# Samples' state products of an mLSTM and a GLA mixer: key and value parts stacked along the contraction, one float32r product of 96 rows in place of row-tiled float32 ones

## The reference, cut to what matters

```
C_new = decay[..., None, None] * C + jnp.einsum('bshd,bshv->bhdv', kw, vc)             # mLSTM
S_new = jnp.exp(BL)[..., None] * S + jnp.einsum('bshd,bshv->bhdv', kc * jnp.exp(BL[:, None] - Bc), vc)   # GLA
```

## Time and profile before

| | |
|---|---|
| median of 3 runs | 2538.49 us (2538.44 to 2538.94) |
| the profiled execution | 2539.21 us, span 2537.4 |
| TensorE busy | 2517.5 us, 99% |
| VectorE busy | 1675.8 us, 66% |
| ScalarE busy | 1072.3 us, 42% |
| products of L1656 (both layers) | 128 records |
| first block of layer 0, of layer 1 | near 568, near 1925 us |

### The profile page before, as it was taken

The page is one execution under the profiler, slowest core; times in us unless marked ns, Lnnn a source line. Parts: engine busy times, 40 slices in busy tenths (PEclk is TensorE's granted clock), DMA queues, the critical chain, the costliest instruction groups (busy, mean ns, idle before and its releaser), DMA issues.

```text
span 2537.4 us, 40969 instructions
## 1 busy us (share of the span) xinstructions
PE 2517.5 (99%) x16901; PEld 2276.0 (90%) x16901; DVE 1675.8 (66%) x2654; ACT 1072.3 (42%) x1568; POOL 0.2 (0%) x4
## 2 busy tenths in 40 slices
PE   9999999999999999999999999999999999999998
PEld 7899898887888999889998998998887988999998
DVE  6744575556457673357764778677876478888886
ACT  5343445442334442454533344446543344433333
POOL 0000000000000000000000000000000000000000
PEclk9999999999999999999999999999999999999999
DMA  6455544535433433453323343344436433333332
GB/s 227 138 173 162 148 150 141 156 110 178 146 102 119 137 96 100 154 170 109 96 84 125 117 135 119 123 155 141 122 106 191 145 129 117 88 100 100 96 100 100
DMA packets 176709, 330.41 MB, mean 130 GB/s; under 512 B 19964, under 2 KB 93436, under 8 KB 176524
## 3 DMA queue, kind: packets, MB, share of 16 engines
q1 hardware_dynamic: 176524, 327.79, 41.2%
HBM read 271.46 MB, written 56.28 MB: 129 GB/s over the span
## 4 chain that ended last, share of the span: by engine, by line
PE 91%; DVE 5%; ACT 2%; issue 1%; DMA 0%; SPq 0%; ACTq 0%; DVEq 0%
PE ps L1192 68%; PE ps L1320 10%; PE ps L1206 3%; PE ps L1570 1%; DVE Y L2438 1%; PE ps L1224 1%; PE ps L1512 1%; PE ps L1656 1%; DVE w_lo L2165 1%; PE ps L1501 1%; PE ps L1495 1%; ACT w_hi L1692 1%; PE ps L1374 1%; PE ps L1494 0%; PE ps L1603 0%
## 5 line engine op out<-in xcount | busy, mean ns | idle before, releaser
L1192 PE MATMUL ps<-HH,w_lo 128*128 128x288 f32 (+1 forms) x2680 | 902.4, 337 | 0.2 <-DVE w_lo L2165 0.2
L1192 PE MATMUL ps<-HL,w_hi 128*128 128x288 f32 (+1 forms) x2680 | 892.2, 333 | 0.0
L1192 PE MATMUL ps<-HH,w_hi 128*128 128x288 f32 (+1 forms) x2680 | 891.8, 333 | 0.0
L2165 DVE TENSOR_TENSOR w_lo<-w_stage,w_hi 128x1024 fp32r<-128x1024 f32 x392 | 478.4, 1221 | 178.3 <-ACT w_hi L1692 177.2
L1192 PEld LDWEIGHTS ps<-HH,w_lo 128*128 128x128 f32 x2680 | 502.9, 188 | 48.8 <-issue 5.8
L1192 PEld LDWEIGHTS ps<-HL,w_hi 128*128 128x128 f32 x2680 | 502.8, 188 | 42.7
L1192 PEld LDWEIGHTS ps<-HH,w_hi 128*128 128x128 f32 x2680 | 503.0, 188 | 41.6
L1692 ACT ACTIVATE w_hi<-w_stage 128x1024 fp32r<-128x1024 f32 x392 | 412.1, 1052 | 295.8 <-PE ps L1192 257.2
L1192 PE MATMUL ps<-hid_hi,w_lo 128*128 128x288 f32 (+1 forms) x1052 | 346.8, 330 | 1.9 <-DVE Y L2438 1.1
L1192 PE MATMUL ps<-hid_lo,w_hi 128*128 128x288 f32 (+1 forms) x1052 | 343.8, 327 | 0.0
L1192 PE MATMUL ps<-hid_hi,w_hi 128*128 128x288 f32 (+1 forms) x1052 | 343.6, 327 | 0.0
(11 more groups left out here) (336 smaller groups left out, 3271.5 us busy)
## 6 DMA issues: line engine op xcount, KB each, us to landing
w_stage<-w_gate_in SPq DMA_DIRECT2D x88, 512.0 KB, 3.7
w_stage<-w_up_in SPq DMA_DIRECT2D x88, 512.0 KB, 3.7
w_stage<-w_down_in SPq DMA_DIRECT2D x88, 512.0 KB, 3.7
w_stage<-w_in_in SPq DMA_DIRECT2D x80, 512.0 KB, 4.1
w_stage<-w_out_in SPq DMA_DIRECT2D x32, 512.0 KB, 3.8
proj_scratch<-evicted SPq DMA_DIRECT2D x48, 288.0 KB, 2.3
proj_scratch<-evicted SPq DMA_DIRECT2D x32, 256.0 KB, 2.1
w_stage<-w_v_in SPq DMA_DIRECT2D x16, 512.0 KB, 4.3
```

The source lines that it names most:

```text
L1192: mm = pe.matmul(ps[:, grp.bank + t, 0:W], wsl(w, k), x[:, k, t * W:(t + 1) * W], start=(k == first and m == 0), stop=(k == last and m == 2))
L2165: dve.tensor_tensor(g.wlo[:, n % NW, :], g.wst[:, n % NW, :], g.whi[:, n % NW, :].bitcast(F32), ALU.subtract).then_inc(s["w_lo"], 1)
```

## The change

Each layer gets two stacks of three thirds of 32 rows: `K4` (high, high, remainder of the weighted keys, for both halves e) and `V4` (high and remainder of the values, so placed that each third of the product is high x high, high x low or low x high). ScalarE makes the high thirds in `key_parts` and `value_parts`, 4 copies each, VectorE the remainders in `prepare(layer, 0)`, 2 and 2. `prepare` masks both halves' stacked keys in one operation per piece, into `k_batch`, whose second buffer lies in `proj_sums`. L1656 becomes one float32r product of 96 rows at full tile per piece and half: 4 per block as before, without a tile position. New waits: ScalarE for its own copies of keys and values, VectorE for all 8 high parts (`parts_hi`) ahead of the remainders and so of the batches of j = 0, TensorE for `parts_lo` ahead of the first L1656 of a layer.

```
--- before.py
+++ after.py
@@ -546,6 +546,8 @@
     g.S1H = sb("s1_hi", [P, 512], F32R)
     s1 = nc.sbuf_base
     g.S1 = sb("s1", [P, 512])
+    g.V4 = nc.alloc_sbuf_tensor_at("v_parts", [3 * 4 * DS, 2, H, DV], F32R, offset=s1 - 3 * 2048)
+    g.K4 = nc.alloc_sbuf_tensor_at("k_parts", [3 * 4 * DS, 2, H, P], F32R, offset=t_end)
     g.S1L = nc.alloc_sbuf_tensor_at("s1_lo", [P, 512], F32R, offset=s1)
     g.Y = [sb(f"Y{b}", [P, KD, NT[b]]) for b in range(2)]
     g.wst = sb("w_stage", [P, NW, 1024])
@@ -554,7 +556,9 @@
     g.hh = sb("hid_hi", [P, 2, NT[1]], F32R)
     g.hl = sb("hid_lo", [P, 2, NT[1]], F32R)
     g.E = sb("evicted", [P, 3, NT[1]])
+    up = nc.sbuf_base
     g.UP = sb("proj_sums", [P, 2, GW[1]])
+    g.KB1 = nc.alloc_sbuf_tensor_at("k_batch_odd", [3 * 4 * DS, 2, 2, P], F32R, offset=up)
     g.C = sb("state", [P, H, DV + 1])
     g.ident = sb("ident", [P, P])
     g.ones = sb("ones", [P, P])
@@ -565,7 +569,7 @@
     g.RC = sb("rstd_column", [P, 4])
     g.mask = sb("mask", [P, L])
     g.mask8 = sb("mask8", [TS, TS])
-    g.bmr = sb("batch_rows", [TS, NB + NB // 2])
+    g.bmr = sb("batch_rows", [3 * 4 * DS, NB + NB // 2])
     g.lmask = sb("level_masks", [P, NLV * L // 2 + L], U32)
     g.reset = sb("reset", [P, L + TS])
     g.bi = sb("bias_if", [H, 2])
@@ -613,7 +617,7 @@
     m.YN = piece("m", "y_normed", [P, H, DV])
     m.TT = piece("m", "y_gated", [P, KD, L])
     m.QB = piece("m", "q_batch", [P, 4, P])
-    m.KB = piece("m", "k_batch", [TS, 4, P])
+    m.KB = piece("m", "k_batch", [3 * 4 * DS, 2, 2, P], dt=F32R)
     m.CS = piece("m", "sample_state", [P, CRING, 2, DV + 1], at["m"])
     at["m"] += 4 * 2 * (DV + 1) * 4
     m.QK = piece("m", "qk", [P, 2 * H, L])
@@ -637,7 +641,7 @@
     x.XL = piece("l", "levels", [P, NLV, H, L])
     x.CS = piece("l", "sample_state", [P, CRING, 2, DV], levels)
     x.QB = piece("l", "q_batch", [P, 4, P], levels + 12288)
-    x.KB = piece("l", "k_batch", [TS, 4, P], 0)
+    x.KB = piece("l", "k_batch", [3 * 4 * DS, 2, 2, P], 0, F32R)
     x.AS = piece("l", "sample_scores", [TS, H, P], 2048)
 
     g.PT = nc.dram_tensor("proj_scratch", [28, P, T], F32, kind="Internal").ap()
@@ -667,7 +671,7 @@
     "n_ready", "spread", "qb_zeroed", "qb", "kb", "b_inter", "b_state", "b_added", "n_saved", "keys_summed", "half_yn", "half_sq", "half_ln", "half_est",
     "half_small", "outs", "y_stored",
 
-    "sums", "s_hi", "s_lo", "t_sum", "t_hi", "t_lo", "prod", "silu", "gated", "p_silu",
+    "sums", "s_hi", "s_lo", "t_sum", "t_hi", "t_lo", "prod", "silu", "gated", "p_silu", "parts_hi", "parts_lo",
 )
 RINGS = (("w_landed", NW), ("x_landed", KD), ("stored", 3), ("c_landed", CRING), ("c_stored", CRING))
 
@@ -681,7 +685,18 @@
     ps = g.ps
     M0 = 4
 
-    BY_ROWS = ((0, 0), (32, 0))
+    def k_batch(layer, j):
+
+        return (g.x if layer else g.m).KB if j % 2 == 0 else g.KB1
+
+
+
+    V_HIGH = ((0, 2), (1, 2))
+    V_LOW = (1, 0)
+
+    def third(r):
+
+        return slice(32 * r, 32 * r + 32)
 
     def normed(N, k):
 
@@ -1627,7 +1642,7 @@
                 if j == NB - 1 and not layer:
 
                     for i in range(H):
-                        mm = pe.matmul(ps[:, M0, 288 + i * NB:288 + (i + 1) * NB], x.KW[0:TS, i, :], g.bmr[:, 0:NB],
+                        mm = pe.matmul(ps[:, M0, 288 + i * NB:288 + (i + 1) * NB], x.KW[0:TS, i, :], g.bmr[0:TS, 0:NB],
                                        start=True, stop=True)
                     mm.then_inc(s["keys_summed"], 1)
                 if j % 2 == 0:
@@ -1649,12 +1664,13 @@
                 mm.then_inc(s["b_inter"], 1)
 
                 pe.wait_ge(s["kb"], 16 * layer + 2 * j + 2)
+                if j == 0:
+                    pe.wait_ge(s["parts_lo"], 4 * layer + 4)
                 wait(pe, s["b_added"], NB * layer + j)
                 for st in (2 * j, 2 * j + 1):
                     for e in range(2):
-                        t = slice(32 * e, 32 * e + 32)
-                        mm = pe.matmul(ps[:, M0 + 2 + e, DV * (st % 2):DV * (st % 2 + 1)], x.KB[t, st % 4, :],
-                                       x.V[t, h, 0:DV], start=True, stop=True, tile_position=BY_ROWS[e])
+                        mm = pe.matmul(ps[:, M0 + 2 + e, DV * (st % 2):DV * (st % 2 + 1)],
+                                       k_batch(layer, j)[:, st % 2, e, :], g.V4[:, e, h, :], start=True, stop=True)
                 mm.then_inc(s["b_state"], 1)
 
             steps = {"last": last, "rstd": rstd, "column": column, "mg4": mgates, "ma": ma, "mv": mv, "mb": mb, "md": md, "me": me, "lg": lgate, "la": la,
@@ -1988,9 +2004,31 @@
                 for h in range(H):
                     ins = act.activation(m.KW[0:n, h, :], heads(2)[0:n, h, :], ACT.Copy, scale=nat(c, 2, h))
                 ins.then_inc(s["k_copied"], 1)
+                if c == NC:
+                    key_parts(0)
+
+            def key_parts(layer):
+
+                act.wait_ge(s["k_copied"], 9 * layer + NC + 1)
+                KW = (g.x if layer else g.m).KW
+                for e in range(2):
+                    for r in range(2):
+                        act.activation(g.K4[third(r), e], KW[third(e), :, :], ACT.Copy).then_inc(s["parts_hi"], 1)
+
+            def value_parts(layer):
+
+                act.wait_ge(s["v_copied"], TURNS(layer, NC))
+                if layer:
+                    act.wait_ge(s["prod"], 5 * len(GROUPS))
+                V = (g.x if layer else g.m).V
+                for e in range(2):
+                    for r in V_HIGH[e]:
+                        act.activation(g.V4[third(r), e], V[third(e), :, 0:DV], ACT.Copy).then_inc(s["parts_hi"], 1)
 
             def mv(c):
                 v_copy(c, 0, g.m.V)
+                if c == NC:
+                    value_parts(0)
 
             def v_copy(c, layer, V):
                 n = SIZE(c)
@@ -2083,6 +2121,9 @@
                 v_copy(c, 1, x.V)
                 act.wait_ge(s["k_turned"], NC + 1 + c + 1)
                 act.activation(x.KW[0:n, :, :], heads(2)[0:n], ACT.Copy).then_inc(s["k_copied"], 1)
+                if c == NC:
+                    value_parts(1)
+                    key_parts(1)
 
             def lb(c):
                 x = g.x
@@ -2863,6 +2904,16 @@
                     dve.wait_ge(s["qb_zeroed"], layer + 1)
                     dve.tensor_copy(x.AS[:, :, :].rearrange("p h (f u) -> p h f u", f=4)[:, :, :, 0:16],
                                     x.A[0:TS, :, 0:TS].rearrange("p h (f u) -> p h f u", f=4)).then_inc(s["spread"], 1)
+                    dve.wait_ge(s["parts_hi"], 8 * layer + 8)
+                    for e in range(2):
+                        dve.tensor_tensor(g.K4[third(2), e], x.KW[third(e), :, :], g.K4[third(e), e].bitcast(F32), ALU.subtract
+                                          ).then_inc(s["parts_lo"], 1)
+                    for e in range(2):
+                        dve.tensor_tensor(g.V4[third(V_LOW[e]), e], x.V[third(e), :, 0:DV], g.V4[third(e), e].bitcast(F32),
+                                          ALU.subtract).then_inc(s["parts_lo"], 1)
+                    if layer:
+                        dve.wait_ge(s["left_dve"], unit("P", 1, 1, GROUPS[-1]).seven.c12)
+                    dve.wait_ge(s["parts_lo"], 4 * layer + 2)
                 for st in (2 * j, 2 * j + 1):
                     h, r = PIECE(st)
                     if j >= 2:
@@ -2876,8 +2927,8 @@
                                     batches(x.QW[:, h, 0:TS], r)).then_inc(s["qb"], 1)
                     if j >= 2:
                         wait(dve, s["b_state"], NB * layer + j - 1)
-                    dve.tensor_scalar(x.KB[:, st % 4, :], x.KW[0:TS, h, :], g.bmr[:, NB + r:NB + r + 1], None, ALU.mult
-                                      ).then_inc(s["kb"], 1)
+                    dve.tensor_scalar(k_batch(layer, j)[:, st % 2, :, :], g.K4[:, :, h, :].bitcast(F32),
+                                      g.bmr[:, NB + r:NB + r + 1], None, ALU.mult).then_inc(s["kb"], 1)
 
             def ss(layer, j):
                 x = g.x if layer else g.m
@@ -2995,7 +3046,7 @@
     after = np.where(s <= l, 0.0, NEG).astype(f)
     s8, l8 = np.arange(TS)[:, None], np.arange(TS)[None, :]
     after8 = np.where((s8 <= l8) & (s8 // DS == l8 // DS), 0.0, NEG).astype(f)
-    batch = np.arange(TS)[:, None] // DS
+    batch = np.arange(3 * 4 * DS)[:, None] // DS
     rows = np.concatenate([batch == np.arange(NB), batch % 4 == np.arange(NB // 2)], 1).astype(f)
     lv = []
     for w in LEVELS:
```

17 lines of the change are left out of this document (11 added, 6 removed).

## The result

Beside each other on one chip the kernel after took 2551.26 us (median of 4 runs, 2549.15 to 2552.54) and the kernel before 2538.72 (4 runs, 2538.44 to 2540.22): a ratio of 1.0045, with a 95% interval of 1.0033 to 1.0057. It is 12.5 us slower, where 7.5 were forecast. Its profiled execution took 2552.5 us, with a span of 2550.8 against 2537.4: 13.4 longer.

The account below looks back on a forecast made before the run. TensorE, busy 99% of the span, was taken to bound the kernel. Layer 0 +3.3, layer 1 +2.0 and the clock +2.2 sum to +7.5 us: 2546.0 us forecast, range 2541.5 to 2550.5.

Parts of the forecast that it names:

- a state block: TensorE, from L1656's first record to the second dense product: 1.41 to 0.82 us, 0.58 taken as saved, 16 blocks.
- ScalarE's copies, a layer: Ahead of each layer's first block: 4 key copies and 4 value copies, 2.15 + 3.85 = 6.0 us.
- VectorE's remainders: In prepare(layer, 0), behind the wait for all 8 copies: 2 key and 2 value remainders, 3.5 us a layer.
- TensorE's wait in layer 0: Ahead of the first block's L1647, which needs the query batches: it begins 7.9 us later than 568.43.
- the low clock in layer 0: After TensorE's idle from 568.7 to 576.3 the granted clock falls to 1.2 GHz, costing 2.2 us.
- layer 1, net: Layer 1's waits less its blocks' savings: 4.9 later with three savings included, five more take 2.9, so +2.0 us.
- the fourth rival: The 96-row product still drains ahead of the dense load (2550.7) or runs in two passes (2553.7); chance 0.08.
- records overlap by 0.1, so 0.54 and 0.96 each: ScalarE's cost per copy: 512 elements take 0.63 us and 1024 take 1.05, less 0.1 of overlap with the neighbouring record.
- three waits: TensorE in layer 1: 1.4 us for a bank's eviction, 3.4 for the query batches, 1.3 for the state sums.
- the tail's 5 us of idleness: At the kernel's end the granted clock falls to 0.50 near 2534.8, after some 5 us without TensorE work.
- the rival with a chance of 0.15: The clock falls in layer 1 too, by the rule of idle gaps over about 3 us: 2548.2 us; chance 0.15.
- the kernel's first products: Nine records from 1.45 to 5.71 took 4.26 us instead of 1.98; 2.2 lost, used as a clock fall's price.

Follow-up runs that it names:

- after2: The changed kernel once more, unaltered, one run for a second trace: 2551.45 us.
- fill: The changed kernel plus products with unread results in TensorE's waits (19 in layer 0, 5 and 6 in layer 1): 2548.88 us, ratio 1.0038 to the kernel before.
- narrow2: The changed kernel with copies and remainders of 2 columns per head, GpSimd clearing the stacks, same products: 2531.82 us, ratio 0.997 to the kernel before.
- l0only: The change in layer 0 alone; layer 1 keeps row-tiled float32 products and has no copies: 2547.37 us, ratio 1.0031 to the kernel before.
- late: The changed kernel with first blocks row-tiled (two in layer 0, four in layer 1), copies and remainders moved later: 2536.45 us, ratio 0.9988 to the kernel before.
- before2: The kernel before once more, unaltered, one run for a second trace: 2539.42 us.
- late2: As late, with layer 0's copies one unit sooner, in an up projection's turn: 2533.61 us, ratio 0.9977 to the kernel before.

## Why the prediction was right, and where its sizes were off

The direction, the places and the mechanism came out as forecast; the sum did not, 12.5 us in place of 7.5, and the median lies 0.8 above the upper end of the range. By steps, in the profiled execution:

| step | forecast | measured |
|---|---|---|
| a state block | 1.41 to 0.82 | 0.81 |
| ScalarE's copies, a layer | 6.0 | 6.9 |
| VectorE's remainders | 3.5 | 3.9 |
| TensorE's wait in layer 0 | 7.9 | 0.98 + 8.29 = 9.3 |
| the low clock in layer 0 | 2.2 | 2.9 (after), 2.3 (after2), both against fill |
| low clock near 1650 | none | 1.3 |
| layer 1, net | +2.0 | +5.5 (after), +4.3 (after2, fill) |
| of that, low clock | none | 0.15 at most |

*The block.* Right in each part: 64 products, 0.12 apart behind the first of a group. One row of the weight loads shows the hand-over: the dense load starts at 587.17, when the last small product starts, without the gap of the earlier trace rows, while the gap ahead of the group is still there ("0.41 <-issue"):

```profile
586.71 0.53 PEld L1672 LDWEIGHTS ps<-v_parts,k_batch_odd 96*128 96x128 f32 x4 [0.41 <-issue]
587.17 0.19 PEld L1207 LDWEIGHTS ps<-hid_hi,w_lo 128*128 128x128 f32 x1
```

So the fourth rival (a drain that stays, or two passes) is out, and the Trainium skill's rule that a change of the tiling mode drains the engine (TensorEngine Tiling (Array Packing), Key Properties) agrees with both gaps, the one gone and the one left. Its rule that small products belong side by side in row groups (TensorE: Matmul & The Clock Gate, Part 3) is outweighed here, as forecast: narrow2, whose only difference from before on TensorE is the stacked form, is 7.7 us faster. The stacked form also halves the passes, and no run compares the two layouts with as many passes each.

*The copies.* This is the term that was mis-sized. The step "records overlap by 0.1, so 0.54 and 0.96 each" took the overlap from two records on 64 and 128 partitions that write different tiles. The four copies of 32 x 1024 take 4.29 us in one record of the view, 1.07 apiece, and the four of 32 x 512 take 2.60, 0.65 apiece, although one of each lasts 1.05 and 0.63: they don't overlap at all. That is 0.9 more a layer, and the remainders (2.46 for two, 1.40 for two) 0.4 more, for the same reason. Together they are 1.3 of the 1.4 us between 7.9 and 9.3. The forecast had also put all of the wait before L1647. In fact 0.98 of it comes earlier, before L1636: the value copy of L2039 stands behind the key copies, and the sample scores' product needs it. That wait moves the place and not the sum, because TensorE would otherwise have waited for the same query batch.

*Layer 1.* The forecast's three waits (1.4 for the bank, 3.4 for the query batch, 1.3 for the state sums) are there: 2.24, then 2.83 in after and 3.92 in after2, and 1.2 in fill alone, where TensorE isn't slowed. What was off is mainly the same term as in layer 0. The bank's wait is longer by the 0.9 of the copies. VectorE goes on from there, and the 0.4 of the remainders comes on top: its query batches and its state sums end 1.4 us behind the forecast's 1931.3 and 1937.3 (1940.62 and 1946.66 in after2, which runs 7.9 behind before by then). Behind the third block the delay is 6.8 in after2 and 6.7 in fill where the forecast had 4.9; 0.5 of that lies in small steps around the blocks that I can't assign. The last five blocks then give 2.5 in place of 2.9, because the wait for l_y_normed ahead of the fifth grew by 0.6. That makes 4.3, and in after 5.5 with the late old state.

The forecast said of the clock "in layer 1 the longest idle is 3.4 us; I take no fall". It fell, at 1931.2, still within the wait of 2.24 us, and again at 1941.4, 0.8 us behind the end of the wait of 2.83. The step that failed there was to take the tail's 5 us of idleness for what a fall needs. But the falls cost 0.15 us at most, by the nets of after, after2 and fill up to the sixth block. So the condition of the rival with a chance of 0.15 came true and its price, 2.2 us, did not: VectorE, not TensorE, sets the time there. The forecast put nothing for this clock and was right only by luck, since its reason was that there would be no fall.

*The low clock in layer 0* cost 2.9 in after where the forecast read 2.2 off the kernel's first products (4.26 less 1.98 is 2.3): it lasted until 582.9, 6.5 us behind the resumption at 576.46, against the 4.3 of those rows. In after2 it lasted 5.1 us behind the resumption and cost 2.3, in l0only 5.4 and 2.4. The mechanism is the forecast's, products at half speed; only the length differs from trace to trace.

*Near 1650* no step of the change stands, and the forecast had nothing there. TensorE waits for VectorE there in every trace, 2.1 us in before, where it was the longest wait, and the clock fell in five of nine traces: after, after2, fill, l0only and late, and not in before, before2, late2 and narrow2. It costs 1.3 to 1.4 us. Neither the stacked products (late2 and narrow2 have them) nor the copies' size (late and late2 have the same) divides the two sets. Nor is it a longer wait: it is 1.92 to 2.00 us in the five traces with the fall and 2.02 to 2.12 in the four without. The cause stays open.

With these corrections 9.3 of wait less 8 x 0.58, and 2.9 for the clock, make 7.6 in layer 0, where 7.8 was measured. The measured parts, 7.8 in layer 0, 1.3 near 1650 and 5.5 in layer 1, less 1.4 for the start, make 13.2 of the 13.4 of span.

## What to carry to other kernels

A rewrite that takes 9 us out of the bounding engine can lose them all in the one moment in which its operands are made: price the making not by the engine's share of the span but by who waits at its end, and put it in a turn where the engine is ahead. Here the same copies turned a gain into 12.5 us of loss in one place; a few units later they cost nothing but the gain of the six blocks that could not wait for them, and one unit further they cost a new wait. Price each wait of TensorE with a possible fall of the clock on top, but only where no other engine is late behind it: in layer 0 the fall cost 2.3 to 2.9 us, in layer 1 next to nothing. And take back-to-back durations for a row of copies, not the spacing of neighbours of another shape.
